# Stick-breaking sums: two one-pass products with a split softplus for the fp32 ones

## The reference, cut to what matters

```python
def stick_breaking_attention(q, k, v):
    """A[t,s] = sigmoid(z_ts) * prod_{s<j<t} (1 - sigmoid(z_tj)), s < t."""
    ...
        z = jnp.einsum('bhqd,bhkd->bhqk', qi, k) * SCALE
        causal = kpos[None, :] < qpos[:, None]
        log_1mb = jnp.where(causal, jax.nn.log_sigmoid(-z), 0.0)
        after = lax.cumsum(log_1mb, axis=3, reverse=True) - log_1mb
        log_a = jnp.where(causal, jax.nn.log_sigmoid(z) + after, NEG)
        return jnp.einsum('bhqk,bhkd->bhqd', jnp.exp(log_a), v)
```

## Time and profile before

| | us |
|---|---|
| median of 3 runs | 3104.14 |
| lowest, highest | 3101.39, 3104.75 |
| the profiled execution, its own time | 3102.03 |
| its span in the trace | 3100.2 |

### The profile page before, as it was taken

One profiled execution on the slowest core, in us unless ns is written; L12 is line 12 of the kernel. 1 busy time (PEld: TensorE's weight loads), 2 busy tenths in 40 slices (PEclk: granted clock), 3 DMA queues, 4 the chain that ended last, 5 costly groups with the idle time before them and its releaser, 6 DMA issues.

```text
span 3100.2 us, 38552 instructions
## 1 busy us (share of the span) xinstructions
PE 3038.8 (98%) x14336; PEld 2516.5 (81%) x14336; DVE 1701.7 (55%) x1802; ACT 1479.5 (48%) x1835; POOL 215.8 (7%) x205
## 2 busy tenths in 40 slices
PE   8999999999999989899999999999999999999999
PEld 7788888888888778788888888888887788888787
DVE  5665455445445775454455444557546555755654
ACT  5554444444445454454444444454555545555553
POOL 0100000000000220000000000004300000510000
PEclk9999999999999999999999999999999999999999
DMA  7456666665556525366666665566544456654455
GB/s 247 154 178 193 188 188 189 190 189 190 190 190 198 150 82 178 116 184 191 188 189 189 190 189 190 189 193 194 151 149 138 149 183 179 188 149 143 143 156 170
DMA packets 278433, 542.12 MB, mean 175 GB/s; under 512 B 16641, under 2 KB 18721, under 8 KB 277665
## 3 DMA queue, kind: packets, MB, share of 16 engines
q1 hardware_dynamic: 276352, 531.30, 56.8%
q0 software_dynamic: 1952, 9.06, 0.8%
HBM read 537.15 MB, written 3.15 MB: 174 GB/s over the span
## 4 chain that ended last, share of the span: by engine, by line
PE 61%; ACT 2%; DVE 1%; issue 0%; ACTq 0%
PE ps L424 15%; PE ps L474 11%; PE ps L907 10%; PE ps L432 8%; PE ps L451 5%; PE ps L914 5%; PE ps L1095 1%; PE ps L1034 1%; PE ps L1073 1%; PE ps L1012 1%; PE ps L741 0%; PE ps L682 0%; PE ps L881 0%; ACT w_hi L366 0%; ACT qkT L1018 0%
## 5 line engine op out<-in xcount | busy, mean ns | idle before, releaser
L373 DVE TENSOR_TENSOR w_lo<-w_raw,w_hi 128x1024 fp32r<-128x1024 f32 x1008 | 1271.2, 1263 | 1322.2 <-ACT w_hi L366 1317.9
L366 ACT ACTIVATE w_hi<-w_raw 128x1024 fp32r<-128x1024 f32 x1008 | 1067.0, 1059 | 1493.9 <-PE ps L432 639.0
L907 PE MATMUL ps<-w_hi,actT_hi 128*128 128x512 f32 x1408 | 550.0, 391 | 0.0
L907 PE MATMUL ps<-w_hi,actT_lo 128*128 128x512 f32 x1408 | 547.9, 389 | 0.0
L914 PE MATMUL ps<-w_lo,actT_hi 128*128 128x512 f32 x1408 | 376.5, 389 | 0.0
L424 PE MATMUL ps<-w_hi,hidT_hi 128*128 128x512 f32 x928 | 363.2, 391 | 1.6 <-DVE hidT_lo L710 1.3
L424 PE MATMUL ps<-w_hi,hidT_lo 128*128 128x512 f32 x928 | 361.2, 389 | 0.0
L474 PE MATMUL ps<-w_hi,actT_hi 128*128 128x512 f32 x832 | 336.5, 404 | 7.2 <-ACT pall L498 5.7
L474 PE MATMUL ps<-w_hi,actT_lo 128*128 128x512 f32 x832 | 325.4, 391 | 0.0
L914 PEld LDWEIGHTS ps<-w_lo,actT_hi 128*128 128x128 f32 x1408 | 264.3, 188 | 55.1
L907 PEld LDWEIGHTS ps<-w_hi,actT_lo 128*128 128x128 f32 x1408 | 264.4, 188 | 54.2
(11 more groups left out here) (276 smaller groups left out, 2707.9 us busy)
## 6 DMA issues: line engine op xcount, KB each, us to landing
w_raw<-ffn_w_in SPq DMA_DIRECT2D x352, 512.0 KB, 3.6
w_raw<-w_in SPq DMA_DIRECT2D x256, 512.0 KB, 3.6
w_raw<-ffn_w_out SPq DMA_DIRECT2D x176, 512.0 KB, 3.8
w_raw<-w_out SPq DMA_DIRECT2D x64, 512.0 KB, 3.9
w_raw<-attn_w_in SPq DMA_DIRECT2D x48, 512.0 KB, 3.7
w_raw<-xattn_w_kv SPq DMA_DIRECT2D x32, 512.0 KB, 4.8
w_raw<-attn_w_out SPq DMA_DIRECT2D x32, 512.0 KB, 3.8
w_raw<-xattn_w_q SPq DMA_DIRECT2D x16, 512.0 KB, 3.7
```

What stands on the lines that cost most here:

```text
L366: nc.scalar.activation(w_hi[:, v % NS], w_raw[:, v % NS], ACT.Copy).then_inc(w_hi_done, 1)
L373: nc.vector.tensor_tensor(w_lo[:, v % NS], w_raw[:, v % NS], w_hi[:, v % NS].bitcast(F32), ALU.subtract).then_inc(w_lo_done, 1)
L907: nc.tensor.matmul(ps[:, 2 * b + tb], lhs[:, k, tb * P:(tb + 1) * P], w_hi[:, s, kk * CB:(kk + 1) * CB], start=(k == 0 and part == 0), sto ...
```

## The change

For each piece VectorE now writes three things: the fp32r part of the softplus into `stW_hi` (two buffers, used in turn), the full softplus into W as before, and the difference of the two, as fp32r, over W (`stW_lo` is `stW`'s memory). The products of `pe_stick_r` take fp32r operands: per head `low_r` with the high part and with the low part over all 384 columns, then all ones with both over the 128 columns that need the second block's keys; four products for three. `low_r` and `ones_r` are fp32r views of the memory of `low` and of the second half of `tri`; VectorE rewrites them in place ahead of `mix1`. Because `tri` is then in two types, the first `lf` product is done in two halves.

```diff
+        stW_lo = at("stW_lo", [4, 384], SCR + 6144, F32R)
+        stW_hi = [at("stW_hi0", [2, 384], SCR + 12288, F32R), at("stW_hi1", [2, 384], SG + 4096, F32R)]
...
+        ones_r = at("ones_r", [P], top[0] - 3 * 512 + 512, F32R)
+        low_r = at("low_r", [P], top[0] - 512, F32R)
...
             for hh in range(2):
 
-                nc.tensor.matmul(ps[:, 2 + hh, 0:256], low[:], W[:, hh, 0:256], start=True, stop=False)
-                nc.tensor.matmul(ps[:, 2 + hh, 128:256], tri[:, P:2 * P], W[:, hh, 256:384], start=False, stop=True)
-                mm = nc.tensor.matmul(ps[:, 2 + hh, 256:384], low[:], W[:, hh, 256:384], start=True, stop=True)
+                parts = (stW_hi[p // 2], stW_lo[:, p:p + 2])
+                for n, part in enumerate(parts):
+                    nc.tensor.matmul(ps[:, 2 + hh, 0:384], low_r[:], part[:, hh], start=(n == 0), stop=False)
+                for n, part in enumerate(parts):
+                    mm = nc.tensor.matmul(ps[:, 2 + hh, 128:256], ones_r[:], part[:, hh, 256:384], start=False,
+                                          stop=(n == 1))
             mm.then_inc(st_r, 1)
...
                 dve.wait_ge(st_ln, 4 * l + q + 1)
-                nc.vector.scalar_tensor_tensor(out=W, in0=Z, scalar=0.0, in1=W, op0=ALU.max,
-                                               op1=ALU.add).then_inc(st_sp, 1)
+                hi = stW_hi[p // 2]
+                vmark(nc.vector.scalar_tensor_tensor(out=hi[:], in0=Z, scalar=0.0, in1=W, op0=ALU.max, op1=ALU.add))
+                vlink(nc.vector.scalar_tensor_tensor(out=W, in0=Z, scalar=0.0, in1=W, op0=ALU.max, op1=ALU.add))
+                nc.vector.tensor_tensor(stW_lo[:, p:p + 2], W, hi[:].bitcast(F32), ALU.subtract).then_inc(st_sp, 1)
...
-                nc.tensor.matmul(ps[0:104, 6, 0:SEQ], lf[:, 0], tri[:], start=True, stop=False)
+                nc.tensor.matmul(ps[0:104, 6, 0:P], lf[:, 0], tri[:, 0:P], start=True, stop=False)
+                nc.tensor.matmul(ps[0:104, 6, P:SEQ], lf[:, 0], ones_r[:].bitcast(F32), start=False, stop=False)
...
             dve.wait_ge(consts_in, 16 * len(CONSTS))
+            vmark(nc.vector.tensor_copy(low_r[:], low[:]))
+            vlink(nc.vector.tensor_copy(ones_r[:], tri[:, P:2 * P]))
             owed["dve"] += dve_norm_steps(dve, "mix1")
```

## The result

The changed kernel takes **3110.65 us**, median of 20 runs (3103.45 to 3115.81); the kernel before, measured beside it in 20 runs, 3100.75 us (3095.96 to 3105.79). The ratio is **1.0029**, 95% interval 1.0021 to 1.0037: slower by 9.0 us (6.5 to 11.5). The forecast was 3108 us within 3102 to 3113, so the time lies in the range; but it is slower by more than 0.2%, where within 0.2% had been given the larger chance. The case that came is the rival "the clock falls behind both waits in both layers".

A forecast was written before the change was run, and what follows sets the result against it. TensorE's own sequence was taken to bound the kernel; +3.5 us from products and softplus and +1.7 us from the clock made +5.2 us, giving 3107.2 on the profiled execution or 3109.3 on the median, put at 3108, range 3102 to 3113 us.

The forecast's parts named there:

- the clock falls behind both waits in both layers: Rival: TensorE's clock falls after the waits at pieces 2 and 3 of each layer; +7.6 us, 3112 us, chance 0.20.
- The products: TensorE's fp32r products take 0.56 us a head instead of 0.88: 0.17 per 384-column product, 0.11 per 128-column one.
- the saving of a piece: Cheaper products on TensorE save 0.63 us in each piece, 5.0 us over eight; bounds 0.19 to 0.79 a piece.
- the lower figure that the prediction set aside: About 81 ns for a sustained weight load and 128-column matmul, from the Trainium skill; 0.11 us was taken instead.
- The dear short product: Rival: 128-column fp32r products cost 0.22 us, as fp32 ones do; +7.0 us, 3111 us, chance 0.07.
- The softplus: VectorE's three instructions for one signal TensorE 1.85 us later; the product starts 2.85 us after the softplus, not 1.00.
- Pieces 0, 1 and 2 of layer 0: TensorE's products start 0.13, 1.06 and 0.5 + 1.85 us later; new waits at pieces 1 and 2 near 1.5 and 2.8.
- Piece 3: Last piece of a layer: products start 2.4 us later, end 1.8 us later; TensorE waits 2.95 us.
- The absorption: VectorE's extra work of piece 2 fits into its 4.42 us wait for ScalarE; two of four pieces pay, +1.75 us a layer.
- The clock: TensorE's granted clock falls once per layer that counts, 1.7 us each; one is already there, so +1.7 us.
- Free, and found free: Copies ahead of `mix1`, the `lf` product cut in two, VectorE's weight splits and `weights` cost TensorE nothing: 0.
- The base: The kernel before at 3102.03 us profiled, 3104.14 us median; the sum gave 3107.2 and 3109.3 on these, forecast 3108.

The follow-up runs named there:

- e6: The changed kernel with the softplus and `weights` steps moved to earlier places in VectorE's order; 3089.66 us, ratio 0.9957 to the kernel before.
- e7: The kernel before with softplus and `weights` steps moved to earlier places in VectorE's order, nothing else; 3087.16 us, ratio 0.9955 to the kernel before.
- e9: The changed kernel run once more, unaltered; 3109.75 us, ratio 1.0025 to the kernel before.
- e5: The changed kernel with three dummy products on TensorE ahead of the softplus wait at pieces 2 and 3; 3102.47 us, ratio 1.0004 to the kernel before.
- e2: The kernel before with VectorE's three softplus instructions for one, the fp32 products unchanged; 3106.17 us, ratio 1.0014 to the kernel before.
- e1: The changed kernel without the low part: one softplus instruction, all four products per head reading the high part; 3099.75 us, ratio 0.9992 to the kernel before.
- e8: The kernel before with three dummy products on TensorE ahead of the softplus wait at piece 3; 3099.39 us, ratio 0.9993.

## Why the prediction was right or wrong, step by step

**The products: 0.56 us a head, right in the sum, wrong in its parts; the saving of a piece 0.05 us too high.** Piece 1 of layer 0 in TensorE's timeline of the changed kernel:

```profile
2335.09 0.44 PE L1289 MATMUL ps<-stW_hi,low_r 128*128 128x384 f32 x1 [1.27 <-DVE stW_lo L1338]
2335.37 0.34 PE L1289 MATMUL ps<-stW_lo,low_r 128*128 128x384 f32 x1
2335.55 0.22 PE L1291 MATMUL ps<-stW_hi,ones_r 128*128 128x128 f32 x1
2335.61 0.27 PE L1291 MATMUL ps<-stW_lo,ones_r 128*128 128x128 f32 x1
2335.72 0.39 PE L1289 MATMUL ps<-stW_hi,low_r 128*128 128x384 f32 x1
2335.94 0.34 PE L1289 MATMUL ps<-stW_lo,low_r 128*128 128x384 f32 x1
2336.12 0.22 PE L1291 MATMUL ps<-stW_hi,ones_r 128*128 128x128 f32 x1
2336.18 0.27 PE L1291 MATMUL ps<-stW_lo,ones_r 128*128 128x128 f32 x1
2336.29 0.45 PE L478 MATMUL ps<-w_hi,actT_hi 128*128 128x512 f32 x1
```

Read the starts: the second head takes 2336.29 − 2335.72 = 0.57 us. Its 384-column product behind a long one is followed after 0.18 us (forecast 0.17), the one behind a short one after 0.22; the first short product after 0.06 and the second after 0.11 (forecast 0.11 each). So the two short ones of a head take 0.17 us together, 0.085 each, and the two long ones 0.40: for the short product alone the lower figure that the prediction set aside was the nearer one, and loading 128 columns of weights is no floor of 0.11 us for each. What was put too high there was put too low for the long ones, and that the two errors cancel is luck. The dear short product (rival, 0.22 us) did not come. The whole piece takes 1.20 us with its restart. I had it save 0.63 us from a price of 2 × 0.88 for the old one; but in the kernel before the next unit starts only 1.67 us after the piece does,

```profile
2324.22 0.59 PE L1283 MATMUL ps<-stW,low 128*128 128x256 f32 x2
...
2325.89 0.48 PE L474 MATMUL ps<-w_hi,actT_hi 128*128 128x512 f32 x1
```

1.78 behind a wait. So a piece saves 1.78 − 1.20 = 0.58 us where it waited before, and 1.67 − 1.20 = 0.47 where only the new one does. Where neither waits it is 0.58 again, for without a wait the new piece takes 2332.14 − 2331.05 = 1.09 us, as piece 1 of e6 shows:

```profile
2331.05 0.33 PE L1289 MATMUL ps<-stW_hi,low_r 128*128 128x384 f32 x1
2331.22 0.34 PE L1289 MATMUL ps<-stW_lo,low_r 128*128 128x384 f32 x1
...
2332.14 0.45 PE L478 MATMUL ps<-w_hi,actT_hi 128*128 128x512 f32 x1
```

This also accounts for the 1.04 us between e6 and e7: four pieces save 4 × 0.58 = 2.32, and e6 gives back its waits of 0.88 us at piece 3 and 0.17 at piece 0 and two restarts of 0.11, which leaves 1.05.

**The softplus: right.** VectorE's timeline of the changed kernel, piece 1:

```profile
2332.22 0.95 DVE L1336 SCALAR_TENSOR_TENSOR stW_hi<-stZ,stW 128x768 fp32r<-128x768 f32 x1
2333.09 0.95 DVE L1337 SCALAR_TENSOR_TENSOR stW<-stZ,stW 128x768 f32<-128x768 f32 x1
2334.08 0.96 DVE L1338 TENSOR_TENSOR stW_lo<-stW,stW_hi 128x768 fp32r<-128x768 f32 x1
```

The starts are 0.87 and 0.99 us apart (forecast 0.86 and 0.98), and TensorE starts 2335.09 − 2332.22 = 2.87 us after the first (forecast 2.85).

**Pieces 0, 1 and 2 of layer 0: right.** Against before, with the 2.55 us of the execution taken off: piece 0 starts 2326.92 − 2324.22 − 2.55 = +0.15 us (forecast 0.13), piece 1 +1.07 (1.06), piece 2 +2.41 (2.35). The waits are 1.27 (forecast 1.5) and 2.77 (2.8). That piece 1's softplus stands for other work and swallows what piece 0 gained was right: of 0.47 us nothing is left.

**Piece 3: right without the clock, wrong with it.** It starts +3.63 us, forecast 2.4. The absorption that the forecast argued for is real. In layer 1 of e9, where no fall came behind piece 2, piece 3 starts 2894.16 − 2891.90 + 0.16 = 2.42 us later than before (the 0.16 because that layer's stretch begins that much earlier). And in e5, where the clock holds, the whole layer costs 1.82 and 1.86, and not the 3 us or more that four paying pieces would. The working with the measured sizes is (1.07 + 1.20 − 1.67) + (1.85 − 0.58) = 1.87. What it left out is what a fall behind piece 2 does to it. ScalarE's and then VectorE's timeline of the changed kernel around piece 3's softplus:

```profile
2371.90 1.06 ACT L370 ACTIVATE w_hi<-w_raw 128x1024 fp32r<-128x1024 f32 x1 [3.38 <-PE ps L455]
```

```profile
2373.06 1.23 DVE L377 TENSOR_TENSOR w_lo<-w_raw,w_hi 128x1024 fp32r<-128x1024 f32 x1 [1.26 <-ACT w_hi L370]
2374.21 0.95 DVE L1336 SCALAR_TENSOR_TENSOR stW_hi<-stZ,stW 128x768 fp32r<-128x768 f32 x1
```

The same split in the kernel before, without idle time ahead of it:

```profile
2368.74 1.22 DVE L373 TENSOR_TENSOR w_lo<-w_raw,w_hi 128x1024 fp32r<-128x1024 f32 x1
```

At 1.2 GHz TensorE ended the unit later, ScalarE waited 3.38 us for it, and the split right ahead of piece 3's softplus waited 1.26 us for ScalarE. The softplus starts at 2374.21; in the kernel before it is 2369.88, and 2369.88 + 2.55 + the 0.5 of the forecast is 2372.93: 1.28 us late, where the rival had put 1.2.

**The clock: this is the step that failed.** "I take one fall per layer that counts, where one in the two layers is in the profiled execution now: + 1.7 us." There were two in each layer, one of them of 3.4 us instead of 1.7. By the record of before, which is one profiled execution, what the falls add to the layers, beyond the clean 1.82 and 1.86, is 3.03 − 1.82 = 1.2 us in layer 0 (its fall behind piece 3 had been there before) and 5.99 − 1.86 = 4.1 in layer 1; in the second execution 1.2 and 2.9. So + 5.3 and + 4.1 us against a forecast of + 1.7, and with the products and the softplus + 9.0 and + 7.7 against + 5.2. The rival's + 7.6 hits the second. The argument I had let count against it, that a fall at piece 2 shortens the wait at piece 3, is true of the changed kernel (2.55, 2.53 and 2.53 us instead of the 2.90 where the clock held; in e2 it is 2.55 us with the fall and without) but does not save anything: falls followed the shorter wait as well in three of the four places where piece 2 had one.

**Free, and found free:** the copies ahead of `mix1`, the cut `lf` product, VectorE's splits and `weights`. No wait of TensorE on any of them shows in the view of waits, apart from the split above, which the clock made late. e1, which has the copies and the cut product, and e8, which has neither, lost the same 18.7 us of clock ahead of the pieces and reach piece 1's scores at 2310.56 and 2310.57: these two cost nothing.

**The base.** The three runs before had a median of 3104.14 us, twenty have 3100.75. With the rise measured as 9.0 us the forecast of 3108 looks closer to 3110.65 than its sum was: the sum is 3.8 us short, and on the base of 3100.75 it would have said 3106. That the time lies so well within the range is in part luck of the base.

## What to carry to other kernels

Where a product waits for VectorE, what was saved on the products ahead of it does not pay: the saving stands in the wait. And an operand that is prepared in more steps ahead of the semaphore is paid in full, once for every piece whose preparation starts on time by itself and not where VectorE had idle time behind it. Ask first where the preparing step stands in the queue; here its place was worth 3.75 us a layer, more than three times what the change brought once the waits were gone. And price an idle wait of TensorE at its length plus the clock it may cost, at every wait in the row and not once, with the spread of both outcomes in the range; a few dummy products in the wait show in one run how much of it is clock.

## What the runs showed of the hardware that I had not expected

- **The same wait has two outcomes.** Over all profiled executions here, a fall to 1.2 GHz followed the wait of 2.77 us at piece 2 in 4 of 6 places, waits of 2.30 to 2.55 us at piece 3 in 4 of 7, waits of 2.89 or 2.90 us in 3 of 3, and of 3.82 or 3.85 us in 2 of 2; none of the waits of the pieces up to 1.4 us was followed by one. e2 has both outcomes for one wait of 2.77 us in its two layers. What decides between them stays open.
- **A fall costs 1.7 or 3.4 us**, nothing between, behind all the waits of the pieces: windows of 6 us at 0.72, of 10 at 0.66 or of 8 at 0.57. Nearly all of it is paid: two layers that are alike but for one fall of 1.7 differ by 1.58 us (before) and by 1.63 (e2). When it is 3.4 and not 1.7 stays open.
- **A short fp32r product** of 128 columns between others costs 0.06 and 0.11 us in turn, and the 384-column one behind it 0.22 where one behind another long one takes 0.17 to 0.18: the short one hands a part of its price on.
- **A restart** behind a wait costs 0.11 us: the first 384-column product is followed after 0.28 us instead of 0.17 (piece 1 of the changed kernel and of e6), the fp32 piece takes 1.78 instead of 1.67 us.
